# The RWKV recurrence of a hybrid trunk, from chunks of 128 tokens to chunks of 64

## The reference

```
def step(S, inp):
    r_t, w_t, k_t, v_t, kk_t, a_t = inp
    sa = einsum('bhvk,bhk->bhv', S, -kk_t)
    S = S * w_t + sa[..., None] * (kk_t * a_t) + v_t[..., None] * k_t
    return S, einsum('bhvk,bhk->bhv', S, r_t)
```

## Time and profile before

| | us |
|---|---|
| median of 3 runs | 2218.3 |
| span of the profiled execution, first to last instruction | 2219.0 |
| TensorE busy | 2094.8 (94%) |
| VectorE / ScalarE / GpSimd busy | 846.1 / 750.9 / 921.4 |
| from the last product of the mixer's bonus sums to the group norm's first product | about 705 to 941.8 |

### The profile page before, as it was taken

One profiled execution on the slowest core, in us unless ns is written; L12 is line 12 of the kernel. 1 busy time (PEld: TensorE's weight loads), 2 busy tenths in 40 slices (PEclk: granted clock), 3 DMA queues, 4 the chain that ended last, 5 costly groups with the idle time before them and its releaser, 6 DMA issues.

```text
span 2219.0 us, 30616 instructions
## 1 busy us (share of the span) xinstructions
PE 2094.8 (94%) x12965; PEld 1677.8 (76%) x12965; DVE 846.1 (38%) x1281; ACT 750.9 (34%) x1090; POOL 921.4 (42%) x423
## 2 busy tenths in 40 slices
PE   5999999989997699998999999899999989989997
PEld 2677877868854578776778778677888868988996
DVE  3323033162258555356230321723033157446123
ACT  1522122263333222246221222622122266456443
POOL 0434443444405121054344434434444444447884
PEclk9999999999998799999999999999999999999998
DMA  9563446223211422243543462264232222224551
GB/s 325 179 205 133 142 134 222 91 94 114 72 43 24 82 49 54 89 140 104 190 146 129 153 229 86 82 218 171 76 114 82 99 82 100 91 77 152 180 174 66
DMA packets 235943, 277.17 MB, mean 125 GB/s; under 512 B 49973, under 2 KB 204611, under 8 KB 235492
## 3 DMA queue, kind: packets, MB, share of 16 engines
q1 hardware_dynamic: 233018, 270.22, 37.3%
q10 hardware_dynamic: 2794, 5.04, 0.6%
HBM read 264.75 MB, written 10.49 MB: 124 GB/s over the span
## 4 chain that ended last, share of the span: by engine, by line
PE 85%; DVE 6%; ACT 4%; DMA 2%; issue 2%; POOL 0%; ACTq 0%; SPq 0%; POOLq 0%; DVEq 0%
PE psum L1155 84%; DVE rs L1989 1%; DMA arena<-in_ada_w 1%; DMA arena<-in_x 1%; ACT arena L807 1%; DVE h L1968 1%; ACTq L719 0%; ACT L869 0%; DVE arena L2077 0%; PE psum L1529 0%; DMA arena<-inverse_kept 0%; ACT arena L1103 0%; DVE h L2036 0%; ACT w_hi L778 0%; DVE arena L2082 0%
## 5 line engine op out<-in xcount | busy, mean ns | idle before, releaser
L2482 POOL TENSOR_TENSOR w_lo<-arena,w_hi 128x1024 fp32r<-128x1024 f32 x332 | 814.5, 2459 | 1015.0 <-ACT w_hi L778 1012.9
L1155 PE MATMUL psum<-u_hi,w_hi 128*128 128x512 f32 (+1 forms) x1888 | 698.8, 370 | 38.8 <-ACT u_hi L807 15.2
L1155 PE MATMUL psum<-u_hi,w_lo 128*128 128x512 f32 (+1 forms) x1888 | 689.4, 365 | 0.0
L1155 PE MATMUL psum<-u_lo,w_hi 128*128 128x512 f32 (+1 forms) x1888 | 675.0, 363 | 0.0
L778 ACT ACTIVATE w_hi<-arena 128x1024 fp32r<-128x1024 f32 x332 | 349.2, 1058 | 735.5 <-PE psum L1155 726.8
L1155 PEld LDWEIGHTS psum<-u_hi,w_hi 128*128 128x128 f32 x1888 | 362.7, 192 | 130.2 <-issue 28.8
L1155 PEld LDWEIGHTS psum<-u_hi,w_lo 128*128 128x128 f32 x1888 | 363.2, 192 | 55.0
L1155 PEld LDWEIGHTS psum<-u_lo,w_hi 128*128 128x128 f32 x1888 | 359.2, 191 | 53.4 <-issue 0.5
L1155 PE MATMUL psum<-arena 64*64 64x64 f32 (+12 forms) x3140 | 277.4, 284 | 23.3 <-DMA arena<-in_hy_f_w 6.2
L1938 DVE TENSOR_TENSOR tmp<-psum,tmp 128x512 f32<-128x512 f32 (+1 forms) x88 | 54.9, 624 | 585.3 <-ACT tmp L832 585.3
L1155 PEld LDWEIGHTS psum<-arena 64*64 64x64 f32 (+5 forms) x3140 | 197.2, 158 | 97.7 <-issue 56.3
(11 more groups left out here) (270 smaller groups left out, 1475.4 us busy)
## 6 DMA issues: line engine op xcount, KB each, us to landing
arena<-in_ada_w SPq DMA_DIRECT2D x48, 1536.0 KB, 6.7
arena<-in_ffn_wg SPq DMA_DIRECT2D x44, 1024.0 KB, 5.3
arena<-in_ffn_wu SPq DMA_DIRECT2D x44, 1024.0 KB, 7.8
arena<-in_ffn_wd SPq DMA_DIRECT2D x20, 2048.0 KB, 7.8
arena<-in_ev_w_in SPq DMA_DIRECT2D x6, 2048.0 KB, 7.7
arena<-in_od_w_in SPq DMA_DIRECT2D x6, 2048.0 KB, 7.9
arena<-in_ffn_wd SPq DMA_DIRECT2D x4, 1024.0 KB, 4.8
arena<-in_ev_w_out SPq DMA_DIRECT2D x2, 2048.0 KB, 9.5
```

The source lines that it names most:

```text
L1155: return pe.matmul(dst, w, x, start=first_, stop=last, skip_group_check=True)
L2482: pool.tensor_tensor(piece_shape(split_lo(pc), src), src, piece_shape(split_hi(pc).bitcast(F32), src), ALU.subtract).then_inc(S("lo_done"), 1)
```

## The change

Chunks are of 64 tokens: eight steps n, and each handles all 16 chains at once. A head's 64 rows lie in one half of the partitions (`rows_of`), so nearly every product is 64x64 in one quadrant of the array.
- Doubling: levels 16 and 32 only (`PE_LEVELS` 2), the results side by side in 32 columns.
- `both_kinds` replaces `rest`: for each head, one product with the key of sa and one with the key of v, over received and read vectors side by side (128 columns), in all four quadrants. VectorE keeps them with `take_factors`. They are made two steps ahead; `turn_keys` too, now 32 small products a step.
- The state passes from every step to the next: `right_side_state`, `right_side_out`, `solve`, then two half copies of the solution (VectorE and ScalarE), `new_state`, and `take_state` on VectorE (addition, scaling). `new_state` stands directly after `solve`, and `take_state` directly after `take_solution`, ahead of `both_kinds(n + 2)` and `take_factors(n + 2)`. `outputs` comes later in the step.
- The values v go to DRAM once and are loaded per step (`load_values`, 4 DMAs). `take_back` is 8 DMAs a step. A lane pass still serves two steps, 32 matrices of 64.
- `hold` is gone. The scans are 8 over 512 tokens, with zeros at the chunk starts.
- ScalarE's `decays_of(2, .)` stand ahead of `z_out(0, 4)`, and `decays_of(3, .)` follow `z_out(3, 5)`.

The diff, cut to its core:

```
+C = 64
+STEPS = NT // C
 LANE_LEVELS = 4
 LANE = 1 << LANE_LEVELS
-PE_LEVELS = LEVELS - LANE_LEVELS
-SQUARE = P * P + P
+PE_LEVELS = 2
...
+        factors = [at.rearrange("p (d e c a t) -> p d e c a t", d=2, e=2, c=CT, a=2)
+                   for at in (arena[:, 4096:6144], arena[:, 6144:8192], arena[:, 2048:4096])]
+        strict_home = arena[:, 38912:39936]
+        stricts = strict_home.rearrange("p (d n c t) -> p d n c t", d=2, n=2, c=CT)
...
+            def take_back(n):
+
+                j, s2 = n // 2, n % 2
+                sp.wait_ge(S("lane_out"), 32 * (j + 1))
+                if n >= 3:
+                    sp.wait_ge(S("s_mm"), n - 2)
+                elif n == 2:
+                    sp.wait_ge(S("bonus_sum"), 4)
+                else:
+                    sp.wait_ge(S("hy_mul"), 4)
+                for k in (1, 0):
+                    for e, rows in enumerate(rows_of):
+                        for d in range(2):
+                            first_ = 64 * (j % 2) + 32 * k + 16 * e + 8 * d + 4 * s2
+                            sp.dma_start(tus[n % 3][rows, k, d], square_rows(inverse_kept, first_, CT))\
+                                .then_inc(S(f"tu_in{n % 3}"), 16)
...
+                lanes_in(0)
+                load_values(0)
+                load_values(1)
+                lanes_back(0)
+                take_back(0)
+                take_back(1)
+                keep_strict(1)
+                lanes_in(1)
+                lanes_back(1)
+                take_back(2)
+                take_back(3)
+                load_values(2)
+                keep_strict(2)
+                lanes_in(2)
+                load_values(3)
+                lanes_back(2)
...
+                for n in range(STEPS):
+                    right_side_out(n)
+                    if n + 1 < STEPS:
+                        z_out(n + 1, 4)
+                    solution_out(n, 1)
...
+                    solution_out(n, 1)
...
+                    if n == 2:
+                        decays_of(3, 0)
+                        decays_of(3, 1)
+                    if n + 2 < STEPS:
+                        keys_out(n + 2)
...
+                def both_kinds(n, d):
+
+                    j, t = n // 2, within(d, n)
+                    if d == 0:
+                        pe.wait_ge(S("k_done"), 4 * n)
+                        pe.wait_ge(S("a_done"), min(STEPS, n + 2 + n % 2) if n >= 2 else 2)
+                        pe.wait_ge(S("slots_1"), 2 + 4 * j)
+                        if n == 0:
+                            pe.wait_ge(S("first_slots"), 7)
                     else:
-                        pe.wait_ge(S("zs"), 2 * (PE_LEVELS * (gi - 3) + 2))
+                        pe.wait_ge(S("k_done"), 4 * n + 2)
+                    for c in range(CT):
+                        for kind, key in enumerate((bk0[j % 2], bk1)):
+                            for e, rows in enumerate(rows_of):
+                                ins = mm(bank[e][rows_of[e ^ kind], c * P:(c + 1) * P], key[rows, d, c, t],
+                                         two_kinds(rows, ar0[j % 3][:, d, c, t], ar1[j % 2][:, d, c, t]), True, True)
+                    ins.then_inc(S("k_mm"), 1)
...
+                def right_side_state(n):
+
+                    j = n // 2
+                    pe.wait_ge(S("state_new"), n)
+                    for i, (d, c) in enumerate(pairs_):
+                        for rows in rows_of:
+                            ins = mm(part_of(5, rows, i, C), ar0[j % 3][rows, d, c, within(d, n)], state[rows, d, c], False, True)
+                    ins.then_inc(S("x_mm"), 1)
...
+                def new_state(n):
+
+                    pe.wait_ge(S("sa_first"), n + 1)
+                    pe.wait_ge(S("sa_second"), n + 1)
+                    pe.wait_ge(S("bkt"), 2 * min(n + 2, STEPS))
+                    for i, (d, c) in enumerate(pairs_):
+                        for e, rows in enumerate(rows_of):
+                            ins = mm(part_of(7, rows, i, C), bkt[n % 2][:, e, d, c], sav[n % 2][:, e, d, c], True, True)
+                    ins.then_inc(S("ns_mm"), 1)
...
+                for n in range(2):
+                    both_kinds(n, 0)
+                    both_kinds(n, 1)
+                    turn_keys(n)
                 strict(2)
                 strict(3)
-                for gi in range(8):
-                    j, hf = gi // 2, gi % 2
-                    ahead = hf == 0 and 0 < j < 3
-                    widen_z(gi, 4)
-                    if gi:
-                        pe.wait_ge(S("tu"), 4 * PE_LEVELS * gi)
-                        hold(4, 2)
-                        right_side(gi - 1)
-                    widen(gi, 4)
-                    if gi:
-                        solve(gi - 1)
-                    widen_z(gi, 5)
+                widen_z(0, 4)
+                widen(0, 4)
+                widen_z(0, 5)
+                widen(0, 5)
+                right_side_values(0)
+                for n in range(STEPS):
+                    more, ahead = n + 1 < STEPS, n + 2 < STEPS
+                    if n:
+                        right_side_state(n)
+                        outputs_state(n)
+                    if more:
+                        widen_z(n + 1, 4)
+                    solve(n)
+                    if more:
+                        new_state(n)
                     if ahead:
-                        strict(gi + 2)
-                        strict(gi + 3)
-                    if gi:
-                        outputs(gi - 1)
-                    widen(gi, 5)
-                    rest(gi, 0)
-                    widen_z(gi, 6)
-                    if hf == 0:
-                        turn_keys(j, 1)
-                    rest(gi, 1)
-                    if hf == 0:
-                        pe.wait_ge(S("zs"), 2 * PE_LEVELS * (gi + 1))
-                        turn_keys(j, 0)
-                        pe.wait_ge(S("bkt"), 4 * j + 2)
-                    if gi == 7:
+                        both_kinds(n + 2, 0)
+                    if more:
+                        right_side_values(n + 1)
+                        widen(n + 1, 4)
+                    else:
+                        pe.wait_ge(S("sa_first"), n + 1)
+                        pe.wait_ge(S("sa_second"), n + 1)
+                    outputs(n)
+                    if not more:
                         gates(0)
-                    widen(gi, 6)
-                    rest(gi, 2)
-                    if gi == 7:
-                        gates(2)
-                right_side(7)
-                solve(7)
-                outputs(7)
-
-                pe.wait_ge(S("o_add"), taken(8))
+                    if more:
+                        widen_z(n + 1, 5)
+                    if ahead:
+                        both_kinds(n + 2, 1)
+                    if more:
+                        widen(n + 1, 5)
+                    if ahead:
+                        turn_keys(n + 2)
+                    if n in (0, 2):
+                        strict(n + 4)
+                        strict(n + 5)
+                gates(2)
...
+                        at = slice(c * NT, (c + 1) * NT)
+                        ve.tensor_tensor_scan(sgw[d][:, at], scan_reset, sgw[d][:, at], 0.0, ALU.mult, ALU.add)\
+                            .then_inc(S("ve_steps"), v.step())
...
+                def take_state(n):
+
+                    ve.wait_ge(S("ns_mm"), n + 1)
+                    st = state.rearrange("p d c v -> p (d c) v")
+                    new = bank[7].rearrange("p (g v) -> p g v", v=C)
+                    scale = carry[:, n].rearrange("p d c -> p (d c)").unsqueeze(2).to_broadcast([P, 2 * CT, C])
+                    if n:
+                        ve.tensor_tensor(st, st, new, ALU.add).then_inc(S("ve_steps"), v.step())
+                        ve.wait_ge(S("ve_steps"), v.n)
+                        ve.tensor_tensor(st, st, scale, ALU.mult).then_inc(S("state_new"), 1)
+                    else:
+                        ve.tensor_tensor(st, new, scale, ALU.mult).then_inc(S("state_new"), 1)
...
+                take_factors(0, 0)
+                take_factors(0, 1)
...
+                for n in range(STEPS):
+                    more, ahead = n + 1 < STEPS, n + 2 < STEPS
+                    take_solution(n, 0)
+                    if more:
+                        take_state(n)
+                    if ahead:
+                        take_factors(n + 2, 0)
+                    if more:
+                        double(n + 1, 4)
+                    take_outputs(n)
+                    if ahead:
+                        take_factors(n + 2, 1)
+                    if more:
+                        double(n + 1, 5)
+                    if n in (0, 2):
+                        take_strict(n + 4)
+                        take_strict(n + 5)
+                    if n in (1, 3):
+                        lane_pairs((n + 3) // 2)
...
+                for j in range(1, 4):
+                    if j == 2:
```

(18 more changed lines are left out.)

803 lines of the change are left out of this document (349 added, 454 removed).

## The result

The changed kernel takes 2194.09 us (median of 4 runs, 2190.46 to 2195.11) beside 2218.21 of the kernel before (2217.72 to 2218.61): ratio 0.9888, 95% interval 0.9874 to 0.9902. It is faster, by 24 us where 21 were forecast. Its runs spread over 4.7 us, those of before over 0.9 here; timed again beside the experiments, the kernel before spread over 6.7 to 9.2 us, so its small spread here says little.

The account below looks back on a forecast made before the run. TensorE's instruction stream plus unfilled waits was taken as the bound. Start, steps, gate products and 6 us of low clock put the group norm's first product at 921 against 941.8, 21 us less: 2198 us, range 2178 to 2229.

Parts of the forecast that it names:

- The start: Before the first step: low clock, lane passes ahead of the second factors and the solution; `new_state(0)` at 770.9 us.
- The steps' ends: Running sum of steps 0 to 5 from 786.4 to 891.8 us, at 18.8 us a step plus waits and extras.
- The prices: TensorE's cost per product: `both_kinds` 103 ns, `widen` 62, `turn_keys` 68; 18.8 us a step, 15.3 to 20.4.
- Lane passes: VectorE's 7.4 us passes ending steps 1 and 3 delay `take_solution`: 2.9 us of wait in steps 2 and 4.
- The decays: ScalarE's `decays_of(3)` behind `z_out(3, 5)`, then GpSimd's multiplications, come late for `strict(6)`: 2.4 us once.
- the values: Loads of v behind the inverse blocks' way back: 1 us put in, at step 5.
- The clock: Four TensorE stretches at the low level, invited by waits and short products: 1.7 us each, 6 us in all.
- The sign that I gave: TensorE's granted clock above 0.93 between 790 and 905 us if right; a mean below 0.86 would show rival 3.
- rival 3: TensorE's clock over the stage stands at 0.80 instead of the assumed 0.96: +30 us, 2228; chance 0.20.
- Rival 1: Four quadrants side by side and 32 columns at 33 ns: 15.3 us a step; inverses' way back returns 10; 2184; chance 0.20.
- Rival 2: Inverse blocks come late; TensorE waits 1 to 4 us in steps 3 and 5, low clock follows: +18, 2216; chance 0.15.
- Edits at nothing: Scans (3.2 us more at most, covered by a wait), `hold` gone, storing v, clearing kept inverses: counted as nothing.

Follow-up runs that it names:

- e10: e9 plus the second pair's strict blocks stored and lanes loaded between the first two inverse sets, lane pass 1 inside step 0's doubling; about 2180 us.
- e1: Changed kernel with the kind of key as outermost loop of `both_kinds` and `turn_keys`, so two quadrants alternate instead of four; the time did not move.
- e5: Changed kernel with GpSimd's last two kinds of decayed keys and receptances of pairs 2 and 3 held until VectorE posts the inverted blocks; 6 us less.
- e8: Changed kernel with lane pass 1, and the last level and posting of passes 2 and 3, behind the state's additions; 8 us worse than the changed kernel.
- e2: Changed kernel with `both_kinds` two steps ahead put back before `new_state`, and `take_factors` before `take_state`; median within 0.4 us of the changed kernel's.
- c0: The changed kernel run again as it is, beside the experiments; about 2195 us.
- e7: e5 with only GpSimd's last two multiplications (second kind of keys) waiting; those on the receptances stand ahead of that wait and the keys' turn; 2190.25 us.
- e3: Changed kernel with SyncE's loads of a pair's first values between the two sets of inverse blocks, not behind both; 7 us less by medians, 6 by ratios.
- e4: Changed kernel with ScalarE's decays of the last pair computed in step 2 ahead of `z_out(3, 5)`; 1.8 us less.
- e9: Changed kernel with the edits of e3, e4 and e7 together; 2181.67 us.
- e6: e8 plus the values' loads between the two sets of inverse blocks; 6 us less than e8 by medians, 0.4% longer than e3 by ratios.
- e11: e10 with the first factors call ahead of the new state in steps 0, 1, 3 and 5; 2175.02 us.

## Why the prediction was right

It was right in the sum and in the first step; in between two errors of some 16 us each cancelled, and that is luck. 2198 were said and 2194.09 measured; the group norm's first product was forecast for 921 and stands at 915.2.

- **The start.** `new_state(0)` at 770.9 forecast, 770.35 measured, by the two large links that were forecast: a lane pass ahead of the second factors (729.5 to 736.9; forecast 728.8 to 736.2), then one ahead of the solution (from 762.3; forecast 762.7). A link between them was another: the doubling of step 0 waits for the inverse blocks (5.19 us ahead of 749.86) and not for `decays_of(2)`, and its copy runs at 751.8 where 754.6 was forecast. The wait of 5.6 us ahead of the new state was avoidable (e10).
- **The steps' ends**, without the clock's share, were forecast for 786.4, 805.2, 831.5, 850.3, 872.0 and 891.8. They came at 784.0, 800.0, 831.4, 846.6, 870.1 and 892.1 (the starts of the next step's products on the state, as 870.08 above). The measured ones hold the clock's share: with the 6 us put in for it the last would be 897.8, 5.7 us later than measured.
- **The prices: too high.** Steps 1 and 3 took 16.0 and 15.2 us where 18.8 stood, the low end of 15.3. Of `both_kinds` (59 ns a product, forecast 103, below both bounds, 68 and 136) and `turn_keys` (33, forecast 68) e1 shows the reason: all four quadrants work side by side, 0.5 and 0.6 us a call. The plain run of step 5 (32 products of 64 columns, 16 of 32) took 58 ns each (870.08 to 872.86, next row the `solve`), not 68 and 62. The run of the doubling, 32 columns, took 59 (904.85 to 907.70, 48 products), 62 taken. So with two quadrants alternating 32 columns cost as much as 64, and the trace agrees with the rule weighed in the prediction, the Trainium skill's TensorEngine Tiling (Array Packing), Instruction Overhead. The load of the weights, 63 ns a product, from which the prediction took its 62, would give the same; no run tells the two apart. The 0.7 us for changes between 64 and 128 rows names no row; in the timeline of before 8 products of 64 by 128 take 1.09 us and 16 take 1.98, which leaves, as an estimate, 0.2 us beyond the products for each such change.
- **The waits: too small**, the term of the sum that was most mis-sized. Lane passes 2.9 us twice forecast; 7.6 and 6.8 beyond the bare wait measured, for two reasons: TensorE's cheaper steps reach the solution sooner, and the pass takes 11.4 us beside GpSimd. I took the pass from a row in which GpSimd was idle. e5 shows 4 us of it. The decays 2.4, measured 4.6; the values 1, measured 3.0. Together 13 us more than forecast, and 4 more for the clock, against 3.3 less in each of five steps for the products.
- **The clock.** Four stretches, 6 us, were forecast. By the rows that stand at both levels steps 2, 4 and 5 lost about 10 (3.3, 2.1 and 4.6; of the last 3.5 in the 158 records and 1.1 in the factors behind them). The sign that I gave, above 0.93 between 790 and 905 us, was wrong: 0.85. Under 0.86 was to mean rival 3, and it did not, as of the some 34 us at the low level between 790 and 905 about 12 lie where TensorE waits. The mean over a stretch with waits was the wrong measure; lengths of equal products at either level are the right one.
- **Rival 1** was nearer to the mechanism than the forecast: its step length of 15.3 held, by its first condition (four quadrants side by side) and against its second (32 columns at 33 ns), and what gave the time back was the lane pass, the decays and the values instead of the way back of the inverses. That one binds as soon as the passes move (e8). **Rival 2** did not occur. **Rival 3** did not.
- **Edits at nothing.** The scans became 1.2 us cheaper. The order ahead of the new state costs the bare wait that stood in the step (0.85, measured 0.78) and buys nothing that e2 shows. `hold`, six times 0.5 us and once 1.0 in the timeline of before, is about 4 of the 24 us; what its removal did to the clock was not tested, as no run puts it back.

The start of the stage (the products of the bonus sums, 703.75 against 701.31) lies 2.4 us later than before, though the change has little ahead of it (the scans, which are shorter). It goes with the clock of the stretch from 50 to 100 us: where that is 0.93, in this execution and those of c0, e2, e7 and e10, the start is 703.7 to 704.0; where it is 1.00, in e3, e4, e5, e8, e9 and before, 700.9 to 701.3 (e6, at 1.00 with 702.3, is the exception). It is part of the spread of 4.7 us. And every run's time is 1.8 us above the span of its profile, so by this estimate the profiled execution of the kernel before took about 2220.8 us, 2.5 above the median and not 0.7.

## What to carry to other kernels

When a change makes the bounding engine's steps shorter, every chain beside it can be late by as much as was saved: write down what each waits for (an issue queue in order, a copy behind another engine's work) with the new step length, not the old. A duration taken from a row is that of the company it had there; ask who is at work beside it in the new schedule. And issue what the next step wants between the parts of a long run of DMAs, not behind it: the orders of e11 bring the kernel to 0.9807 of the one before, the change alone to 0.9888.

## What the runs showed of the hardware

- VectorE's operation on 8 elements lasts 1.13 to 1.23 us instead of 0.17 while GpSimd multiplies SBUF tensors (the changed kernel against e5).
- 64x64 products in all four quadrants: 33 ns at 64 columns and 59 at 128; with two quadrants alternating 52 and 89 (e1).
- Behind a wait for the values the same 158 to 160 records took 8.0 to 8.6 us in the seven places where it was 2.4 to 3.9 us, and 4.9 to 5.0 in the seven where it was 0.4 to 1.7; behind 1.24 us in step 6 148 took 4.60 (e5, e9) or 8.08 (e11). A gap can cost its length and as much again. These kernels spread by 3 to 12 us from run to run, the kernel before by 1 to 9.
- SyncE takes 0.7 to 0.8 us for each issue of an inverse block of 64 KB, 11 to 12.7 us for a pair: a transfer's place in that list moved the kernel by 6 to 7 us (e3), where the order on TensorE moved nothing that e2 shows.
